# The second phase of a split feed-forward layer: three loads for the sums, the pieces of x and two waits change their places on SyncE's queue

## The reference, cut to what matters

```python
h = rmsnorm(x, norm2_g[l])
x = x + (jax.nn.silu(h @ w_gate[l]) * (h @ w_up[l])) @ w_down[l]
```

## Time and profile before

| | |
|---|---|
| median of 3 runs | 2378.61 us (2375.26 to 2378.81) |
| time of the profiled execution | 2373.76 us |
| its span in the trace | 2371.9 us |
| TensorE busy | 2293.5 us, 97% of the span |
| granted clock of TensorE, mean | 0.992 |
| last pair's last product ends, second phase begins | near 2139.7 us of the span |
| second phase ends | near 2365 us |

### The profile page before, as it was taken

How to read it: one execution, slowest core, us unless ns; L and a number is a source line. 1 busy time by engine, 2 the same in 40 slices (tenths; PEclk the granted TensorE clock), 3 DMA queues, 4 the chain that set the end, 5 groups by cost and what they waited for, 6 DMA issues and landing times. The chain is left out here.

```text
span 2371.9 us, 28672 instructions
## 1 busy us (share of the span) xinstructions
PE 2293.5 (97%) x10508; PEld 1850.3 (78%) x10508; DVE 1414.2 (60%) x1814; ACT 950.7 (40%) x1529; POOL 605.7 (26%) x450
## 2 busy tenths in 40 slices
PE   6999998999999999999999999999999999998999
PEld 5788886686888888888887777776778888886887
DVE  6468357637644544454547469995485555555685
ACT  5332257635322122222234458884343333334433
POOL 1120044432000000000004506662264544433310
PEclk9999999999999999999999999999999999999999
DMA  9256532122211111111122331002323323229976
GB/s 340 64 162 225 184 90 67 77 69 92 71 36 53 44 53 44 53 44 53 45 91 94 114 96 39 27 9 98 100 83 114 122 85 116 98 103 338 338 261 225
DMA packets 238907, 261.77 MB, mean 110 GB/s; under 512 B 13433, under 2 KB 175561, under 8 KB 238289
## 3 DMA queue, kind: packets, MB, share of 16 engines
q1 hardware_dynamic: 236128, 252.82, 32.0%
q0 software_dynamic: 2208, 7.37, 0.9%
q10 hardware_dynamic: 465, 0.17, 0.0%
HBM read 204.72 MB, written 55.61 MB: 110 GB/s over the span
## 5 line engine op out<-in xcount | busy, mean ns | idle before, releaser
L303 PE MATMUL ps<-hhi,whi 128*128 128x512 f32 x1056 | 415.1, 393 | 6.8 <-DVE arena L3310 3.5
L305 PE MATMUL ps<-hhi,wlo 128*128 128x512 f32 x1056 | 412.2, 390 | 0.0
L304 PE MATMUL ps<-hlo,whi 128*128 128x512 f32 x1056 | 412.1, 390 | 0.0
L776 POOL TENSOR_TENSOR cbuf<-cbuf 128x512 f32<-128x512 f32 (+1 forms) x50 | 74.2, 1492 | 851.4 <-ACT cbuf L763 848.8
L227 DVE TENSOR_TENSOR wlo<-raw,whi 128x1024 fp32r<-128x1024 f32 x116 | 151.6, 1310 | 201.0 <-ACT whi L222 201.0
L303 PEld LDWEIGHTS ps<-hhi,whi 128*128 128x128 f32 x1056 | 198.9, 188 | 50.5 <-DVE arena L3310 3.9
L304 PEld LDWEIGHTS ps<-hlo,whi 128*128 128x128 f32 x1056 | 199.0, 188 | 42.5 <-issue 1.2
L305 PEld LDWEIGHTS ps<-hhi,wlo 128*128 128x128 f32 x1056 | 198.9, 188 | 41.5
L2694 DVE SCALAR_TENSOR_TENSOR cbuf<-ps,par,cbuf 128x1023 f32<-128x1023 f32 x44 | 56.4, 1282 | 226.5 <-ACT cbuf L2602 226.5
L1740 POOL TENSOR_TENSOR cbuf<-cbuf,attn_stats 128x1024 f32<-128x1024 f32 x80 | 151.5, 1894 | 95.5 <-DVE attn_stats L2001 95.5
L222 ACT ACTIVATE whi<-raw 128x1024 fp32r<-128x1024 f32 x116 | 120.4, 1048 | 128.7 <-PE ps L2578 118.3
(11 more groups left out here) (438 smaller groups left out, 5197.0 us busy)
## 6 DMA issues: line engine op xcount, KB each, us to landing
raw<-in_w_up SPq DMA_DIRECT2D x56, 512.0 KB, 3.8
shared<-hidden_blocks SPq DMA_DIRECT2D x77, 256.0 KB, 5.2
raw<-in_w_in SPq DMA_DIRECT2D x32, 512.0 KB, 4.9
arena<-in_w_ada SPq DMA_DIRECT2D x32, 512.0 KB, 5.4
lead_work<-in_w_down SPq DMA_DIRECT2D x55, 256.0 KB, 4.6
arena<-in_w_down SPq DMA_DIRECT2D x50, 256.0 KB, 3.8
x_park<-arena SPq DMA_DIRECT2D x6, 2048.0 KB, 9.2
raw<-in_w_down SPq DMA_DIRECT2D x22, 512.0 KB, 3.2
```

Of the source, the lines that this page charges most:

```text
L303: nc.tensor.matmul(acc[:, tok], whi[:, s, ws], hhi[:, k, tok], start=(k == 0), stop=False)
L304: nc.tensor.matmul(acc[:, tok], whi[:, s, ws], hlo[:, k, tok], start=False, stop=False)
L305: mm = nc.tensor.matmul(acc[:, tok], wlo[:, s, ws], hhi[:, k, tok], start=False, stop=(k == DK - 1))
```

## The change

It touches the second phase alone.

- `load_down_rows(q)` stands behind unit 3 + 3q in place of unit 7 + 3q, and `store_down_sums(q - 1)` with it. In front of the first one the queue waits for the first product of the last j in place of its last one. The buffers `rows3` and `second` are other blocks, so that this is allowed.
- `store_hidden(10)` stands ahead of unit 9, before ahead of unit 7. `store_hidden_sums(10)` stands ahead of unit 12, before ahead of unit 10. The wait for the landed hidden blocks stays ahead of unit 10.
- The 16 pieces of x stand behind the units in `X_UNITS`: 12, 14, 16, 18, then 34 to 41, then 45, 47, 49, 51. Before they stood behind the odd units 11 to 41. The wait for the last product stands ahead of the first piece.
- On GpSimd `pool_down(0)` stands ahead of `pool_hidden(10)`, before behind it.

```diff
+            X_UNITS = (12, 14, 16, 18) + tuple(range(3 * Q + 1, 3 * Q + 9)) + (45, 47, 49, 51)
...
-                self.second = [over_lo[:, 7, half(0)], over_lo[:, 7, half(1)], over_lo[:, 0, half(0)], over_lo[:, 1, half(0)]]
-                self.rows3 = [[over_lo[:, k, half(h)] for k, h in at3]
-                              for at3 in (((4, 0), (4, 1), (5, 0)), ((5, 1), (6, 0), (6, 1)))]
+                self.second = [over_lo[:, 4 + i, half(0)] for i in range(4)]
+                self.rows3 = [[over_lo[:, i, half(0)] for i in range(3)],
+                              [over_lo[:, 3, half(0)], over_lo[:, 3, half(1)], row_hi[:, at:at + HALF]]]
...
                 for u in range(self.UNITS):
-                    if u == 7:
+                    if u == 9:
                         self.store_hidden(sp, self.Q - 1)
-                    if u == self.Q - 1:
+                    elif u == self.Q - 1:
+                        sp.wait_ge(F["stored"], 48 * self.Q)
+                    elif u == self.Q + 1:
                         self.store_hidden_sums(sp, self.Q - 1)
-                        sp.wait_ge(F["stored"], 48 * self.Q)
-                    if u == 2 * self.Q:
+                    elif u == 2 * self.Q:
                         sp.wait_ge(F["tstored"], 64 * self.Q)
                     self.load_unit(sp, u)
-                    q, turn = divmod(u - 7, 3)
+                    q, turn = divmod(u - 3, 3)
                     if turn == 0 and 0 <= q < self.Q:
                         if q == 0:
-                            sp.wait_ge(F["mm"], 7 * (self.PAIRS - 2))
+                            sp.wait_ge(F["mm"], 7 * (self.PAIRS - 3) + 1)
                         self.load_down_rows(sp, q)
                     if turn == 0 and 0 < q <= self.Q:
                         self.store_down_sums(sp, q - 1)
-                    if u >= self.Q and u % 2 and u < self.Q + 32:
-                        i, n = divmod((u - self.Q) // 2, 4)
+                    if u in self.X_UNITS:
+                        if u == self.X_UNITS[0]:
+                            sp.wait_ge(F["mm"], 7 * (self.PAIRS - 2))
+                        i, n = divmod(self.X_UNITS.index(u), 4)
...
+                self.pool_down(pool, 0)
                 self.pool_hidden(pool, self.Q - 1)
-                for q in range(self.Q):
+                for q in range(1, self.Q):
                     self.pool_down(pool, q)
```

## The result

The changed kernel takes 2383.81 us (median of 7 runs, 2379.92 to 2386.79), the kernel before 2375.59 (7 runs, 2373.14 to 2378.81). The ratio is 1.0032, 95% interval 1.0019 to 1.0044: **slower by some 7.6 us**. The time lies in the predicted range (2373 to 2385), and 2.5 us from the predicted 2381.3. But that stood on a median of before of 2378.61; as a difference, +2.75 us and "within 0.2%" were the likeliest case, and the time lost is nearly three times that.

What follows compares the result with a forecast made beforehand. The prediction took TensorE's one stall at unit 11, set by unit 16's landing, to bound the second phase. Its terms 0.45 + 1.6 + 0.7 gave +2.75 us, 2381.3 us on a median of 2378.61; range 2373 to 2385.

Steps and rivals of the forecast that it cites:

- within 0.2%: Whole kernel: the stall stays, unit 16 lands between 2.6 us earlier and 3.75 us later; likeliest case, chance 0.73.
- One stall, worth what the landing of unit 16 says: TensorE at unit 11: 8.8 us plus 1.7 us of clock loss; the time moves one for one with the landing.
- The clock term: TensorE behind the stall at unit 11: 1.7 us lost at the low clock, taken to stay.
- the rival: Stall at unit 11: short enough to keep the clock, saving 5.1 us, or gone, saving 10.5 us; chance 0.11.
- Blocks counted against a hole, +0.45: SyncE's queue ahead of unit 16: four blocks less save 2.6 us, a silent queue costs 3.1 us.
- "slower" rival: Unit 16's load waits behind rows and sum of q = 3: up to 2.4 us on top, +5.15 us; chance 0.14.
- The sum of q = 0 beside VectorE, +1.6: Ahead of the last hidden product: GpSimd's moved sum slows VectorE's subtractions, 1.6 us on a chain without slack.
- The hidden sums beside VectorE, +0.7: GpSimd's last hidden sums beside VectorE's splits of units 7 and 8: 6.1 us for 5.4, lengthening the queue's wait.
- The pieces of x, 0: Loads beside units 34 to 41 and 45 to 51: hidden by ScalarE's lead, cost 0; without that cover 2.6 us.
- The sum: Whole kernel: 0.45 + 1.6 + 0.7 = +2.75 us, or 2381.3 us on the median, +0.12%.
- the changed profile: Expected signs: one TensorE wait of 9 to 12 us at line 3631, and a queue silent for some 4 us.

Runs made afterwards that it cites:

- down1_first: The changed kernel with GpSimd's sum of q = 1, too, ahead of the last hidden sums; ratio to the kernel before 1.0002.
- no_sum0: The changed kernel with GpSimd's two instructions for q = 0 left out, so those blocks are stored unsummed; ratio to the kernel before 1.0012.
- down1_x_back: The kernel of down1_first with the pieces of x behind the odd units 13 to 43; ratio to the kernel before 1.0003.
- late_rows_sum0: The kernel of late_rows with GpSimd's sum of q = 0 ahead of the last hidden sums again; ratio to the kernel before 1.0000.
- x_behind_16: The kernel before with the pieces of x behind units 17 to 26 and odd units 27 to 37, none ahead of unit 16; ratio 0.9994.
- late_rows: The changed kernel with rows from q = 2 behind units 17 to 37, no GpSimd sum ahead of the last hidden ones, x from unit 18; ratio to before 0.9989.
- x_alone: The kernel before with only the pieces of x moved to the changed kernel's units; ratio to the kernel before 0.9996.
- x_back: The changed kernel with the pieces of x back behind the odd units 11 to 41; ratio to the kernel before 1.0024.
- hidden_twice: The changed kernel with one more GpSimd subtraction of 128x512 at the head of the last four hidden sums; ratio to the kernel before 1.0032.
- late_rows_adds: The kernel of late_rows with VectorE's additions for pass 5 ahead of unit 71 in place of unit 72; ratio to the kernel before 0.9986.

## Why the prediction was right, and where it was off

- **One stall, worth what the landing of unit 16 says.** Right: the landing moved by 5.0 us, TensorE's resumption by 5.1. The clock term was called constant; it grew by 1.1 us, as TensorE worked 5.7 us at 1.2 GHz behind this stall and 3.4 behind the other. It doesn't follow the stall's length: 2.9 us behind 9.4 (down1_first), 3.4 behind 12.4 (no_sum0), 6.1 behind 9.8 (down1_x_back). Nor is the fall at 5.4 us a limit below which a stall keeps the clock, as the rival had it: late_rows_sum0 lost it in 2.3 us.
- **Blocks counted against a hole, +0.45.** The hole is there, opened by the wait named. As a rule the count failed: x_behind_16 has three blocks less and gains 0.5 us for an expected 1.9, since the ring of four held unit 16 as well. In the kernel before the two were 0.2 us apart, and the prediction counted only the blocks. For the changed kernel the second burst took 23.5 us for 22.85, which is near; its last link is the rows, sum and store of q = 3, as the "slower" rival had it, at a price of 0.65 and not 2.4. That is less than the rival's own rule gives: the rows of q = 3 landed 13.8 us into the burst for a reckoned 11.1, which with its 1.0 us of slack would be 1.7. So the near fit of the burst is luck in part.
- **The sum of q = 0 beside VectorE, +1.6.** Right in place and kind, measured +2.2; no_sum0 gives back 1.6 of it at the store, and late_rows_sum0 against late_rows 1.7.
- **The hidden sums beside VectorE, +0.7.** The mis-sized term: +1.7. Only the four hidden sums were reckoned beside VectorE. The two instructions of the sum of q = 1 met it as well (1.74 and 1.62 us in place of 1.28), and the queue waits for all six: 9.9 us, where the prediction had 8.2 without a collision (2154.35 - 2146.15) and 8.9 with its 0.7. That 2154.35 is itself 0.16 us more than its terms add up to (2151.54 + 2.65). VectorE's three units were stretched in their turn, so it was there all the while.
- **The pieces of x, 0.** Not refuted: x_alone is 0.9996. The wait of 1.6 us at the transposes was not foreseen, and only the profiled execution of the changed kernel shows it at that size; it varies (0 in x_back and no_sum0, 1.1 in x_alone).
- **The sum.** +2.75 predicted; +8.0 in the trace, of which 2.25 more on the landing, 1.1 clock, 1.6 transposes. The direction and the two collisions were right; "within 0.2%", to which it gave 0.73, was wrong, as these extras are of one sign. That the time lies in the range is luck in part. The range stood on a median of 2378.61, and seven executions of the kernel before have 2375.59; moved by that much it would end at 2382, under the measured 2383.81. Nor does the changed profile look as foretold in size: a stall of 13.7 us for 9 to 12, a silent queue of 5.8 us for some 4.

## What to carry to other kernels

A wait placed behind loads is free only if its releaser's own engine has nothing in front of it: read that engine's program order, not the time at which the data land. Here one instruction order of GpSimd cost more than all the moved transfers were worth. A count of transfers is a bound only while nothing else in the chain waits: look at what else the transfer waited for, here a place in a ring of four. And before a stall is removed, look for the next bound behind it: of 10.5 us only some 3 were to be had, because another chain stood 2.1 us away.

## What the runs showed of the hardware that was not expected

- Two engines that both read two SBUF operands went one for one: from 2148.39 on VectorE started five subtractions at a step of 1.70 us in place of 0.60, and GpSimd five instructions at about the same step (2147.93 to 2154.81), each 1.62 to 1.74 us long in place of 1.29. The Trainium skill, "SBUF — State Buffer", section "Who interferes with whom", says that issue order decides who blocks; in this trace both lose.
- TensorE's clock fell 5.4 us after the last matmul in the kernel before, and some 2.4 us after it in the changed one, near 2170.4; in the other ten traces in which it fell, 2.0 to 2.8 us after it. In late_rows_sum0 it fell in a stall of 2.3 us, in late_rows_adds it held through one of 1.8. Behind the stalls of 7.7 us and more TensorE worked 2.9 to 6.1 us at 1.2 GHz before the full clock came back.
- The issue of a DMA on SyncE's queue, 0.43 us as a rule, lasted 1.65 us at 2160.27 in the changed kernel (194 GB/s in that window), 2.25 us in hidden_twice (220 and 75 GB/s in the two windows that it spans) and 1.51 us at 2163.87 in down1_x_back, where the DMA engines moved 394 to 405 GB/s. So it doesn't go with low traffic alone, and no run tells why.
- 256 KB took 3.3 to 8.1 us from issue to landing in the stretch of the earlier trace rows, most of it with full DMA engines, and 8.3 us at the longest in x_behind_16. A ring of four loaded blocks is then a bound of its own: unit 16 waited for unit 12's split in x_behind_16, and by 0.2 us in the kernel before.
